# Gathers of u and v rows issued in alternating pairs in an expert layer on GpSimd

## The chip, the cores and the metric

The kernel runs on one core of one Trainium2 chip. The metric is device time in microseconds (us) of one launch. The engines are named as in the profile: PE (TensorE, matmul), DVE (VectorE), ACT (ScalarE), POOL (GpSimd), SP (SyncE, which issues the plain DMAs). Each runs its own list of instructions in program order, and they meet at semaphores.

## The reference

One block over 1024 tokens of width 1024, float32: an input projection, gated delta-net heads and sliding-window attention heads, an output projection, then a layer of single-neuron experts, then a gated per-layer embedding. The change lies in the expert layer (PEER). For each token, 8 heads pick 16 of 16384 experts each, 128 in all:

```python
def peer_experts(xn, w_query, sub_keys, expert_u, expert_v):
    ...
        eid = e1 * PEER_NKEYS + e2
        gate = jax.nn.softmax(sc, axis=-1)
        hid = jnp.einsum('thkd,td->thk', expert_u[eid], xb, preferred_element_type=f32)
        act = jax.nn.gelu(hid, approximate=False) * gate
        return jnp.einsum('thk,thkd->td', act, expert_v[eid].astype(f32)).astype(xb.dtype)
```

So for every token and each of its 128 experts one row of `expert_u` and one of `expert_v` (1024 floats each, 4 KB) are needed. That is 2 x 1024 x 128 rows, 1073.7 MB.

## The kernel before, in words

**Tiles and groups.** The tokens are cut into 8 tiles of 128, one token a partition. The 128 experts of a token are cut into 16 groups of 8 (`G = 8`, `NG = 16`). One gather (an indirect DMA) brings, for one expert slot, one row for each of the 128 tokens: 512 KB. A group has 8 gathers from `table_u` into `u_ring` (128 x 8 x 1024) and 8 from `table_v` into `v_ring`. Each ring holds one group: slot j of the next group goes where slot j of this one was.

**What is done with a group.**
- POOL, `gather_group` (L562 to L576): copies the 8 indices of each token into `ids` (L567), then issues the gathers (L576). Before an even slot it waits until the row before in that slot and the next has been used (L574), on `u_used` for u rows and `v_used` for v rows.
- DVE, `experts` (L1642 to L1648): for each slot j it waits for `u_landed[j]`, multiplies the u row by the token's input and sums it (L1645, one fused instruction, called a reduction here), which raises `u_used`. After the eighth it waits for ACT's gelu and multiplies by the gates (L1648).
- ACT, `experts`: the gelu, then eight diagonal matrices (`weight_diagonals`, 128 x 128), one for each slot, with the weights of the 128 tokens on the diagonal. Each waits for `v_used` of the slot's last user.
- PE, `experts` (L1169 to L1181): for each slot it waits for `v_landed[j]` and for the diagonal, then multiplies the diagonal by the v row in two halves (L894), into the sum `expert_sum` in PSUM. A group is 32 matmul records. Every slot raises `v_used`.

**The two halves of a tile.** While the experts of tile t-1 are computed, the same engines compute everything ahead of the experts for tile t (the "front": delta-net, attention, projections, the choice of experts), cut by hand into 16 pieces. The orders are written out by hand, and they differ by engine:

```python
# DVE, tile(t)                       # PE, tile(t)
for g in range(NG):                  for g in range(NG):
    experts(t - 1, g)                    if g:
    if g == 0:                               experts(t - 1, g - 1)
        experts_out(t - 2)               pieces[g](t)
    pieces[g](t)                     experts(t - 1, NG - 1)
publish(t)
```

ACT has DVE's order (experts of group g, then piece g). So DVE and ACT are one group ahead of PE: beside PE's experts of group g-1 stand their experts of group g, and piece g is shared by the three engines after these. Most pieces go to and fro between PE, ACT and DVE; piece 9 on PE is a projection (16 of its matmuls, `w_out_sb`) with no input from DVE or ACT in the same piece, and pieces 14 and 15 have nothing on PE. The eighth tile's experts run beside the embedding at the end (`normed_rows`, `result`, `take_pT` on DVE, `turn_rows`, `gate`, `project_p` on PE; DVE's L1718 and L1721 are in `result`).

**What sets POOL's order.** Only the code of `gather_group`, called for group after group. POOL has nothing else to do but take over the indices of a tile (`take_ids`). Where it waits for a slot, each later gather waits behind it. SP's queue has the loads of weights and of the tile's inputs and isn't touched by the change.

Of the kernel before, what the change touches and what calls it, by code (L numbers as in the profile page):

```python
# [55 lines left out]
G = 8  # L56
# [50 lines left out]
def block_kernel(nc, x, p, g_mix, w_in, gdn_conv_w, gdn_a_log, gdn_dt_bias, gdn_norm_g, swa_q_norm_g, swa_k_norm_g,  # L107
# [4 lines left out]
    sub_keys, table_u, table_v = peer_sub_keys[0], peer_u[0], peer_v[0]  # L112
# [8 lines left out]
    with ExitStack() as ctx:  # L121
        def signal(name):
            return ctx.enter_context(nc.semaphore(name))
# [51 lines left out]
        u_used = signal("u_used")  # L175
        u_landed = [signal(f"u_landed{u}") for u in range(G)]
        v_used = signal("v_used")
        v_landed = [signal(f"v_landed{u}") for u in range(G)]
# [87 lines left out]
        def sb(where, name, shape, dt=F32):  # L266
            return where.enter_context(nc.sbuf_tensor(name, shape, dt))
# [34 lines left out]
        with ExitStack() as b_ctx:  # L302
# [4 lines left out]
            u_ring = sb(b_ctx, "u_rows", [P, G, D])  # L307
            v_ring = sb(b_ctx, "v_rows", [P, G, D])
# [15 lines left out]
            ids = sb(b_ctx, "group_ids", [P, 2, G], U32)  # L324
# [236 lines left out]
        @block.gpsimd  # L561
        def _(pool):  # L562
            def gather_group(t, g, half):

                n = t * SLOTS + g * G
                first = isinstance(g, int) and g == 0 and isinstance(t, int)
                nc.gpsimd.tensor_copy(ids[:, half, :], eid[:, bass.ds(g * G, G)]).then_inc(group_ids_ready, 1)  # L567
                pool.wait_ge(group_ids_ready, t * NG + g + 1)
                pool.sem_inc(wait_carrier)
                for table, ring, used, landed in ((table_u, u_ring, u_used, u_landed), (table_v, v_ring, v_used, v_landed)):  # L570
                    for j in range(G):
                        if j % 2 == 0 and not first:

                            pool.wait_ge(used, n - G + j + 2)  # L574
                            pool.sem_inc(wait_carrier)
                        nc.gpsimd.indirect_dma_start(  # L576
                            ring[:, j, :], None, table, bass.IndirectOffsetOnAxis(ids[:, half, j:j + 1], 0)).then_inc(landed[j], 16)

            def take_ids(t):

                pool.wait_ge(vector_front, t + 1)
                pool.sem_inc(wait_carrier)
                nc.gpsimd.tensor_copy(eid[:], eid_new[:]).then_inc(ids_taken, 1)
                pool.wait_ge(ids_taken, t + 1)

            pool.wait_ge(first_ids_ready, 1)
            nc.gpsimd.tensor_copy(eid[:, 0:EARLY * G], eid_new[:, 0:EARLY * G]).then_inc(first_ids_taken, 1)  # L589
            pool.wait_ge(first_ids_taken, 1)  # L590
            for g in range(EARLY):
                gather_group(0, g, g % 2)
            take_ids(0)
            with pool.Fori(EARLY // 2, NG // 2) as pair:
                g = pair * 2
                for half in range(2):
                    gather_group(0, g + half, half)
            with pool.Fori(1, NT) as t:
                take_ids(t)
                pool.sem_inc(wait_carrier)  # L600
                with pool.Fori(0, NG // 2) as pair:
                    g = pair * 2
                    for half in range(2):
                        gather_group(t, g + half, half)
# [1156 lines left out]
```

## Time and profile before

| What | Value |
|---|---|
| Time, median of 3 runs | 4106.42 us (4103.27 to 4132.05) |
| Span of the profiled execution | 4090.1 us |
| The median run above that span | 16.3 us |
| PE busy | 3315.7 us, 81% |
| DVE busy | 2191.8 us, 54% |
| ACT busy | 992.4 us, 24% |
| POOL busy | 2278.2 us, 56% |
| DMA moved | 1214 MB, of which 1073.87 MB are the gathers |

The profile is of one execution. No time of that execution as a whole is given beside its span, so the runs' median stands for it: 16.3 us lie around the span. Expert work begins some 520 us into the span, when the first front is done, and takes the rest of it. Busy shares are means over pieces with different limits. A row of the time line gives start, duration, engine, line, operation, and in brackets how long the engine had been idle and who ended that. PE records of one kind in a row are merged, and the start of a merged row is that of its first instruction.

### The profile page before, as it was taken

Reading aid. Unit: us, or ns where it says so; the run is one execution under the profiler, and the core shown is the slowest. Engines: PE = TensorE matmul, PEld = TensorE weight load, DVE = VectorE, ACT = ScalarE, POOL = GpSimd, SP = SyncE. Lnnn points to the kernel's source line nnn. Section 1 sums busy time; section 2 is a strip of 40 time slices with the busy share of each in tenths; the row PEclk is TensorE's granted clock in tenths of the full one; section 3 lists DMA queues with packets and bytes.
Section 4 is the critical chain, followed back from the end, with each engine's and each line's share of the span. In section 5 each row is a group of like instructions: output and inputs, shape, how many; then the busy total and the mean of one; then the engine's idle time right before and its main releaser. Section 6 shows DMA issues by size and latency. Waiting matters only on the chain.

```text
span 4090.1 us, 38210 instructions
## 1 busy us (share of the span) xinstructions
PE 3315.7 (81%) x11032; PEld 1816.9 (44%) x11032; DVE 2191.8 (54%) x4881; ACT 992.4 (24%) x2278; POOL 2278.2 (56%) x2189
## 2 busy tenths in 40 slices
PE   8997757897788787887879778877888687969999
PEld 4444535453444344443535344444545253534444
DVE  1124285567444854477456744486357644574543
ACT  2112213222222132212221222212221222213332
POOL 0000055667556775767566755676566656666764
PEclk9998778898889897898889888898899798989999
DMA  3321187899789998899889978899799979999996
GB/s 125 118 75 63 39 298 263 309 363 389 264 302 335 362 358 289 316 346 365 280 313 373 365 269 297 318 360 342 278 324 369 356 260 322 352 364 373 381 355 243
DMA packets 413927, 1214.00 MB, mean 297 GB/s; under 512 B 43680, under 2 KB 137888, under 8 KB 413600
## 3 DMA queue, kind: packets, MB, share of 16 engines
q0 software_dynamic: 294912, 1073.87, 71.6%
q1 hardware_dynamic: 118816, 137.66, 9.9%
q8 instruction: 103, 1.69, 0.2%
q14 instruction: 96, 0.79, 0.1%
HBM read 1190.61 MB, written 20.77 MB: 296 GB/s over the span
## 4 chain that ended last, share of the span: by engine, by line
PE 54%; DVE 14%; issue 13%; DMA 7%; POOL 5%; ACT 4%; another core or an unknown queue 2%; SPq 1%; POOLq 0%; DVEq 0%; ACTq 0%
PE expert_sum L894 28%; PE bank L894 23%; DVE u_rows L1645 5%; DMA u_rows<-in_peer_u_dram,group_ids 4%; DMA w_query<-in_peer_w_query_dram 3%; PE bank L897 3%; POOL u_rows L576 3%; POOL v_rows L576 2%; ACT weight_diagonals L610 1%; ACT L610 1%; ACT arena L610 1%; DVE arena L1420 1%; DVE arena L1552 1%; DVE arena L1537 1%
## 5 line engine op out<-in xcount | busy, mean ns | idle before, releaser
L894 PE MATMUL expert_sum<-v_rows,weight_diagonals 128*128 128x512 f32 x4096 | 1871.7, 617 | 153.0 <-ACT weight_diagonals L610 116.9
L576 POOL DMA_INDIRECT v_rows<-in_peer_v_dram,group_ids x1024 | 1191.1, 1163 | 827.7 <-PE expert_sum L894 541.8
L1645 DVE CUSTOM_DVE_ANT_0 u_rows<-u_rows,ffn_in 128x1024 f32<-128x1024 f32 x1024 | 1215.7, 1225 | 454.8 <-DMA u_rows<-in_peer_u_dram,group_ids 410.3
L894 PEld LDWEIGHTS expert_sum<-v_rows,weight_diagonals 128*128 128x128 f32 x4096 | 810.4, 200 | 1161.7 <-issue 1078.0
L576 POOL DMA_INDIRECT u_rows<-in_peer_u_dram,group_ids x1024 | 1052.3, 1028 | 416.8 <-issue 371.0
L897 PE MATMUL bank<-constants,arena 128*128 128x128 f32 x968 | 184.5, 336 | 330.2 <-DVE arena L1475 82.4
L610 ACT ACTIVATE weight_diagonals<-constants,expert_weight 128x128 f32<-128x128 f32 x1024 | 331.7, 390 | 228.5 <-PE expert_sum L894 177.4
L894 PE MATMUL bank<-w_query,arena 128*128 128x256 f32 (+1 forms) x1088 | 297.6, 436 | 87.4 <-DMA w_query<-in_peer_w_query_dram 50.6
L610 ACT ACTIVATE gelu<-hidden 128x8 f32<-128x8 f32 x128 | 26.7, 208 | 1386.1 <-DVE hidden L1645 1237.0
L897 PEld LDWEIGHTS bank<-constants,arena 128*128 128x128 f32 x968 | 139.1, 171 | 392.6 <-issue 212.2
L894 PEld LDWEIGHTS bank<-w_query,arena 128*128 128x128 f32 x1088 | 231.6, 215 | 155.7 <-issue 59.6
L589 POOL CAST expert_id<-expert_id_new 128x32 uint32<-128x32 f32 x1 | 0.2, 209 | 522.1 <-DVE expert_id_new L1602 522.1
L894 PE MATMUL bank<-arena 128*128 128x128 f32 (+4 forms) x2176 | 252.2, 295 | 40.1 <-issue 23.0
L894 PEld LDWEIGHTS bank<-arena 128*128 128x128 f32 (+3 forms) x2176 | 240.7, 201 | 60.5 <-issue 47.0
L894 PE MATMUL bank<-w_out_sb,arena 128*128 128x512 f32 x512 | 235.2, 615 | 21.9 <-ACT arena L861 10.4
L610 ACT ACT_TABLE_LOAD x172 | 220.7, 1283 | 3.8 <-PEq L1751 0.7
L1420 DVE COPY_PREDICATED arena<-constants,bank 128x512 f32<-128x512 uint32 x80 | 58.1, 726 | 287.3 <-PE bank L894 131.6
L894 PE MATMUL bank<-normed_by_channel,w_channel 128*128 128x512 f32 x384 | 167.2, 598 | 0.5 <-issue 0.5
L894 PEld LDWEIGHTS bank<-w_out_sb,arena 128*128 128x128 f32 x512 | 99.5, 197 | 146.7 <-issue 132.7
L894 PE MATMUL bank<-w_token,normed_tile 128*128 128x512 f32 (+1 forms) x384 | 142.4, 532 | 0.0
L1513 DVE TENSOR_TENSOR arena<-arena,bank 128x512 f32<-128x512 f32 x16 | 11.0, 688 | 203.5 <-PE bank L894 173.0
L894 PEld LDWEIGHTS bank<-normed_by_channel,w_channel 128*128 128x128 f32 x384 | 73.7, 193 | 93.6 <-issue 93.6
(166 smaller groups left out, 1968.1 us busy)
## 6 DMA issues: line engine op xcount, KB each, us to landing
w_query<-in_peer_w_query_dram SPq DMA_DIRECT2D x64, 1024.0 KB
u_rows<-in_peer_u_dram,group_ids POOLq DMA_INDIRECT x1024
v_rows<-in_peer_v_dram,group_ids POOLq DMA_INDIRECT x1024
w_channel<-in_w_in_dram SPq DMA_DIRECT2D x12, 512.0 KB
conv_scratch<-conv_out SPq DMA_DIRECT2D x12, 512.0 KB, 2.6
arena<-conv_scratch SPq DMA_DIRECT2D x8, 768.0 KB
tok_scratch<-token_out SPq DMA_DIRECT2D x8, 648.0 KB
arena<-tok_scratch SPq DMA_DIRECT2D x8, 648.0 KB
```

The lines of the kernel that those rows point to most:

```text
L576: nc.gpsimd.indirect_dma_start(ring[:, j, :], None, table, bass.IndirectOffsetOnAxis(ids[:, half, j:j + 1], 0)).then_inc(landed[j], 16)
L589: nc.gpsimd.tensor_copy(eid[:, 0:EARLY * G], eid_new[:, 0:EARLY * G]).then_inc(first_ids_taken, 1)
L610: return nc.scalar.activation(out_, in_, func, **kw)
L894: return nc.tensor.matmul(out_, lhsT, rhs, start=start, stop=stop, **kw)
L897: return nc.tensor.transpose(out_, in_, ident)
L1420: v.copy_predicated(invT[:, 4 * r:4 * r + 4, :], level_mask(l), bank[3 + r][:, :].rearrange("p (s n) -> p s n", n=P)).then_inc(invT_ready, 1)
L1513: v.tensor_tensor(h1[:, n * 512:n * 512 + 512], x_t[:, n * 512:n * 512 + 512], bank[n][:, :], ALU.add).then_inc(h1_ready, 1)
L1537: last = v.max_index(index[:, first], top[:, first], row)
L1552: last = v.max_index(index[:, second], top[:, second], row)
L1645: v.tensor_tensor_reduce(u_ring[:, j, :], u_ring[:, j, :], xb[:], 1.0, 0.0, ALU.mult, ALU.add, hid[:, g * G + j:g * G + j + 1]).then_inc(u ...
```

## The change

The two loops in `gather_group` change places. Before, POOL issued the 8 gathers of u rows and then the 8 of v rows, with a wait for used slots ahead of each pair. Now it goes over the four pairs of slots, and for each pair issues two u rows and then two v rows, each two behind the same wait as before. The number of gathers, their sizes, the semaphores and the values waited for are the same. No other engine's instructions change.

```diff
-                for table, ring, used, landed in ((table_u, u_ring, u_used, u_landed), (table_v, v_ring, v_used, v_landed)):
-                    for j in range(G):
-                        if j % 2 == 0 and not first:
+                for j in range(0, G, 2):
+                    for table, ring, used, landed in ((table_u, u_ring, u_used, u_landed), (table_v, v_ring, v_used, v_landed)):
+                        if not first:
 
                             pool.wait_ge(used, n - G + j + 2)
                             pool.sem_inc(wait_carrier)
-                        nc.gpsimd.indirect_dma_start(
-                            ring[:, j, :], None, table, bass.IndirectOffsetOnAxis(ids[:, half, j:j + 1], 0)).then_inc(landed[j], 16)
+                        for i in range(j, j + 2):
+                            nc.gpsimd.indirect_dma_start(
+                                ring[:, i, :], None, table, bass.IndirectOffsetOnAxis(ids[:, half, i:i + 1], 0)).then_inc(landed[i], 16)
```

On POOL, in the loop over the groups of a tile, one group of before (`group_ids` is `ids`, `in_peer_u_dram` is `table_u`):

```order
L567 COPY group_ids<-expert_id 128x8
L568 ISA
L574 ISA
L576 DMA u_rows<-in_peer_u_dram,group_ids 128x1024 x2
L574 REGISTER_ALU
L576 DMA u_rows<-in_peer_u_dram,group_ids 128x1024 x2
L574 REGISTER_ALU
L576 DMA u_rows<-in_peer_u_dram,group_ids 128x1024 x4
L576 DMA v_rows<-in_peer_v_dram,group_ids 128x1024 x8
```

On POOL, the same group in the changed kernel (the gather's line is L577 there):

```order
L567 COPY group_ids<-expert_id 128x8
L568 ISA
L574 ISA
L577 DMA u_rows<-in_peer_u_dram,group_ids 128x1024 x2
L577 DMA v_rows<-in_peer_v_dram,group_ids 128x1024 x2
L574 REGISTER_ALU
L577 DMA u_rows<-in_peer_u_dram,group_ids 128x1024 x2
L577 DMA v_rows<-in_peer_v_dram,group_ids 128x1024 x2
L574 REGISTER_ALU
L577 DMA u_rows<-in_peer_u_dram,group_ids 128x1024 x2
L577 DMA v_rows<-in_peer_v_dram,group_ids 128x1024 x2
```

These eleven rows reach to the third pair; the fourth follows in the same way. The first pair of v rows, and the wait on `v_used` ahead of it, has moved ahead of six gathers of u rows; the last gather of u rows is now the twelfth behind that wait, itself included.

## Rows read from the trace of the kernel before

**Rows 1.** The page: its span, and part 4, the chain that ended last
```profile
span 4090.1 us, 38210 instructions
...
PE 54%; DVE 14%; issue 13%; DMA 7%; POOL 5%; ACT 4%; another core or an unknown queue 2%; SPq 1%; POOLq 0%; DVEq 0%; ACTq 0%
PE expert_sum L894 28%; PE bank L894 23%; DVE u_rows L1645 5%; DMA u_rows<-in_peer_u_dram,group_ids 4%; DMA w_query<-in_peer_w_query_dram 3%; PE bank L897 3%; POOL u_rows L576 3%; POOL v_rows L576 2%; ACT weight_diagonals L610 1%; ACT L610 1%; ACT arena L610 1%; DVE arena L1420 1%; DVE arena L1552 1%; DVE arena L1537 1%
```

**Rows 2.** The page, part 5: busy us, mean ns | idle before, and most of it
```profile
L576 POOL DMA_INDIRECT v_rows<-in_peer_v_dram,group_ids x1024 | 1191.1, 1163 | 827.7 <-PE expert_sum L894 541.8
```

**Rows 3.** Waits of the whole span: us in total, times, longest us
```profile
POOL v_rows L576 <- PE expert_sum L894: 541.8, 195, 22.7
...
DVE u_rows L1645 <- DMA u_rows<-in_peer_u_dram,group_ids: 410.3, 216, 13.3
```

**Rows 4.** Time line of PE, expert bursts of the tile from 1898 us
```profile
1898.06 13.90 PE L894 MATMUL expert_sum<-v_rows,weight_diagonals 128*128 128x512 f32 x32
...
2018.70 15.06 PE L894 MATMUL expert_sum<-v_rows,weight_diagonals 128*128 128x512 f32 x32
2042.16 15.30 PE L894 MATMUL expert_sum<-v_rows,weight_diagonals 128*128 128x512 f32 x32
2074.79 15.96 PE L894 MATMUL expert_sum<-v_rows,weight_diagonals 128*128 128x512 f32 x32
...
2130.55 13.90 PE L894 MATMUL expert_sum<-v_rows,weight_diagonals 128*128 128x512 f32 x32
2151.15 13.90 PE L894 MATMUL expert_sum<-v_rows,weight_diagonals 128*128 128x512 f32 x32
...
2335.82 4.44 PE L894 MATMUL expert_sum<-v_rows,weight_diagonals 128*128 128x512 f32 x7
```

**Rows 5.** Time line of POOL, gathers at three places of that tile
```profile
2012.58 0.94 POOL L576 DMA_INDIRECT u_rows<-in_peer_u_dram,group_ids  x1 [0.30 <-issue]
2024.27 0.94 POOL L576 DMA_INDIRECT v_rows<-in_peer_v_dram,group_ids  x1 [10.74 <-PE expert_sum L894]
2025.51 0.94 POOL L576 DMA_INDIRECT v_rows<-in_peer_v_dram,group_ids  x1 [0.30 <-issue]
...
2060.28 1.99 POOL L576 DMA_INDIRECT v_rows<-in_peer_v_dram,group_ids  x1 [0.30 <-issue]
...
2134.96 1.94 POOL L576 DMA_INDIRECT v_rows<-in_peer_v_dram,group_ids  x1 [2.91 <-PE expert_sum L894]
```

**Rows 6.** Time line of DVE, the last reduction of two groups
```profile
2021.17 1.22 DVE L1645 CUSTOM_DVE_ANT_0 u_rows<-u_rows,ffn_in 128x1024 f32<-128x1024 f32 x1
...
2061.38 1.22 DVE L1645 CUSTOM_DVE_ANT_0 u_rows<-u_rows,ffn_in 128x1024 f32<-128x1024 f32 x1
```

**Rows 7.** Two windows: us, busy by engine (x instructions), PEclk, DMA share, GB/s
```profile
2074.80:2090.80 16.00, 16.00 (x34) 6.75 (x34) 8.79 (x18) 4.56 (x11) 6.00 (x6) 0.87 0.96 331
...
1898.10:2335.80 437.70, 350.76 (x1222) 195.80 (x1221) 257.59 (x585) 105.77 (x259) 286.69 (x272) 0.89 0.92 331
```

**Rows 8.** Time lines of POOL and DVE: a group's last u gather, then its reduction
```profile
2107.13 1.49 POOL L576 DMA_INDIRECT u_rows<-in_peer_u_dram,group_ids  x1 [0.30 <-PE expert_sum L894]
...
2112.88 1.22 DVE L1645 CUSTOM_DVE_ANT_0 u_rows<-u_rows,ffn_in 128x1024 f32<-128x1024 f32 x1 [0.66 <-DMA u_rows<-in_peer_u_dram,group_ids]
...
2211.46 1.75 POOL L576 DMA_INDIRECT u_rows<-in_peer_u_dram,group_ids  x1 [0.30 <-issue]
...
2222.97 1.23 DVE L1645 CUSTOM_DVE_ANT_0 u_rows<-u_rows,ffn_in 128x1024 f32<-128x1024 f32 x1 [0.35 <-DMA u_rows<-in_peer_u_dram,group_ids]
```

**Rows 9.** Time lines of PE and DVE, two groups of the last tile
```profile
3742.77 13.90 PE L894 MATMUL expert_sum<-v_rows,weight_diagonals 128*128 128x512 f32 x32
3755.57 1.23 DVE L1721 TENSOR_TENSOR arena<-arena 128x1024 f32<-128x1024 f32 x1
3765.51 13.90 PE L894 MATMUL expert_sum<-v_rows,weight_diagonals 128*128 128x512 f32 x32
...
3789.55 13.90 PE L894 MATMUL expert_sum<-v_rows,weight_diagonals 128*128 128x512 f32 x32
```

## The prediction

> **What bounds the kernel now.** I read the page first. Of its span of 4090.1 us the chain that ended last lies 54% on TensorE (PE) and 14% on VectorE (DVE) [rows 1]. No engine is full; the bound is a chain between engines, and busy shares say little about a moved wait. Among the costliest groups stand the 1024 gathers of v rows on GpSimd (POOL), mean 1163 ns, and before them 541.8 us of 827.7 idle for PE's expert matmuls [rows 2]. 128 groups of 8 experts pass through POOL, DVE and PE. The waits say who holds whom: POOL stood those 541.8 us, in 195 waits, at v slots that PE had not used up, and DVE 410.3 us, in 216, at u rows that had not landed [rows 3]. So in the old order POOL stands still at v rows, **after** all u rows of that group are on their way.
>
> Then one tile in the order of time. Call T the start of a group's 32 expert matmuls on PE. Between 1898.06 and 2335.82 there are 16 such starts, of which the first, the last period's end and five between are shown: 437.8 us in 16 periods of 14 to 38 us [rows 4]. While PE works at group n from T = 2018.70, DVE already reduces the u rows of group n+1: their last gather was issued at 2012.58, before T, and the last reduction is over at 2022.39, 3.7 us after T [rows 5, 6]. POOL then stands 10.74 us, until 2024.27, which is T + 5.57, for the first v slots, and after the next v gather goes on at 1.24 us each [rows 5]. DVE is one group ahead of PE, and the eight early u gathers are what allows it.
>
> PE, DVE and ACT each run "experts of group n+1 (or n), then piece n+1 of the next token tile" in program order. DVE's and ACT's share of a piece stands behind their expert work of group n+1. So the next T comes a tail after the later of two ends: PE's burst, or DVE's last reduction of group n+1.
>
> **The change part by part.** It removes no gather and adds none: 16 a group stay, as do the four waits on u slots and the four on v slots. Only POOL's order changes: u0 u1, v0 v1, u2 u3, and so on. The first v wait moves ahead of six u gathers. Behind it on POOL now stand those six; for them waits DVE (the reductions of group n+1), behind DVE the gelu, the gates and the diagonals on ACT, and behind these both engines' piece. SP's queue isn't touched.
>
> When is DVE's last reduction of group n+1 over, counted from T? Four terms, whose sum I call D.
> - First v slots free: 5.6 us (2018.70 to 2024.27) [rows 4, 5]. It depends on PE's pace: behind the burst of 13.90 us the first v gather starts at T + 4.4 (2130.55 to 2134.96) [rows 4, 5], and a burst of 15.96 us had a mean granted clock of 0.87, between the levels of 1.2 and 2.4 GHz [rows 4, 7]. PE will idle more after the change, so I take the slower value and keep 4.4 as the lower bound.
> - From there u7 is the twelfth gather: v0 v1 u2 u3 v2 v3 u4 u5 v4 v5 u6 u7. Eleven steps of 1.24 and one of 0.94 make 14.6 us [rows 5].
> - Beside a reduction a gather takes 1.99 us in place of 0.94 [rows 5, 6]: 1.05 more. Six u rows are reduced while these twelve are issued, which gives 0 to 6.3 us; I take half, 3.0, since pairs land 5 us apart and a pair is reduced in 2.3.
> - From the end of u7's issue to the end of its reduction: 5.5 us where the queue was short (2108.62 to 2114.10), 11.0 where it was long (2213.21 to 2224.20) [rows 8]. POOL will have stood still ahead of these, so DMA is drained: 5.5.
>
> D = 5.6 + 14.6 + 3.0 + 5.5 = **28.7 us**. The lower end is 4.4 + 14.6 + 0 + 5.5 = 24.5, the upper 5.6 + 14.6 + 6.3 + about 7 = 33.5. The four later v waits cost nothing: PE uses up a pair each 3.5 to 4 us and POOL comes by each 5.
>
> On the third term the Trainium skill has a rule: "SBUF — State Buffer", section "Who interferes with whom", says that a VectorE instruction with two SBUF inputs contends with a GpSimd one that reads SBUF and that the loser blocks fully. The rows of 1.99 beside 0.94 agree. By the rule in full the term is 6.3 rather than 3.0; it is the second rival below.
>
> Now the tails, tile of rows 4, from the later end to the next T. Where a piece needs DVE or ACT the tail stays; where it is PE's alone it runs during the wait, and only gelu, gates and first diagonal remain: 1.0 us, as in the fourteenth and fifteenth group, which have nothing else. In order: 14.4, 14.2, 13.2, 19.0, 8.4, 12.2, 2.2, 16.4, 1.0, 16.9, 7.2, 7.1, 9.7, 1.0, 1.0, 5.3, together 149.2 us. Three of them in rows: the fifth is 2033.76 to 2042.16; the sixth runs from DVE's end at 2062.60 to 2074.79; the ninth was 6.7 us of PE alone (2144.45 to 2151.15) and falls to 1.0 [rows 4, 6].
>
> One group keeps its end: the fifteenth, whose reductions start late behind DVE's own piece and end 30.7 us after T. A tile then takes 15 x 28.7 + 30.7 + 149.2 = 610.4 us in place of 437.8: **+173**. Six tiles run so: 6 x 173 = 1038. In the last tile a pair of groups takes 22.7 + 24.0 = 46.8 us (3742.77 to 3789.55) [rows 9]. The second becomes D + 1.0 = 29.7, since what follows its burst is PE's alone; the first becomes D + 3 + 8.8 = 40.5, as PE's first transpose there waits for DVE's last product, L1721, some 3 us behind the reductions (over at 3756.80, when the burst ended too), and 8.8 us of PE and ACT follow, to 3765.51 [rows 9]. That is +23.4 a pair, seven pairs: 165. The first tile has two groups that DVE holds up anyway; I take 150 for the rest. Sum: 4090.1 + 1038 + 150 + 165 = 5443 us of span. The median run of before lies 16.3 us above the profiled span, so **5460 us**.
>
> Why no cover is left: DMA, busy 0.92 at 331 GB/s in that tile [rows 7], is the one resource near its limit. It is filled in the old order because POOL queues eight u rows ahead of its stand at v. With the stand behind two u rows the queue drains each time, and the same bytes at a tile of 610 us make 331 x 438/610 = 238 GB/s.
>
> **The rivals.**
> 1. *Faster*: u rows no longer lie in the DMA queue behind eight v rows. DVE's 410.3 us at DMA would go; the chain has 4% of the span at that wait, 164 us [rows 1, 3], so 4106 - 164 = 3942 us. It wins where the DMA queue holds a u row longer than POOL's wait for PE does. For it: issue to reduction took 11.0 us behind a full queue [rows 8]. Against: POOL's 10.74 us stand now comes ahead of six u rows and outweighs the 5.5 us that a short queue saves, in each period.
> 2. *Still slower*: each reduction blocks a gather in full, 6.3 in place of 3.0. D = 32.0, 15 x 3.3 = 50 us more a tile and about 8 tiles: 5860 us.
> 3. *No change*: v slots are free by the time POOL comes to them, so that the order doesn't matter: 4106. Against it: 195 waits, 541.8 us in all [rows 3].
> 4. *Mild*: pieces start during the wait after all, and only groups whose period is under D pay (seven of the sixteen, by 7.5 us in the mean): 52 a tile, some 440 us with the first and last tile, 4550 us. Against it: DVE's and ACT's pieces stand behind the delayed reductions in program order.
>
> **How the numbers follow.** The forecast has 0.85, rival 2 0.07, rival 4 0.04, rival 1 0.02, rival 3 0.02. What a measurement of this kernel tells from no change is about 1%. Slower by over 1%: 0.85 + 0.07 + 0.04 = 0.96, I say 0.95; within 1%: 0.03; faster: 0.02. The lower end takes D = 24.5 and 15 us a tile less in tails, since PE's first matmuls of a piece run ahead: +95 a tile, 570 + 90 + 110 = 770, so about 4870; the upper end takes D = 33.5, +245 a tile, 1470 + 190 + 220 = 1880, about 5980. I give 4850 to 5950.
>
> **What would show it.** Right: POOL's largest wait sits still at v rows for PE, with longer stands, and just ahead of them only two u rows; DVE's wait for u rows grows from 410 us to over 1000, its last reduction ending 25 to 33 us after T; PE idles about 14 us after nearly every burst; DMA falls to some 240 GB/s; GpSimd's mean gather rises above 1163 ns. Wrong: DVE's last reduction before T + 20, or shares of DMA near 0.9. If D is right and the time isn't, the tails were wrong, the granted clock first.

## The result, and the profile after

The changed kernel takes **5278.1 us** (median of 4 runs, 5249.39 to 5299.24) and the kernel before 4108.36 us (4103.27 to 4132.05) beside it: a ratio of 1.281, with a 95% interval of 1.275 to 1.287. The forecast was 5460 us in a range of 4850 to 5950. The growth is 1170 us where 1354 were forecast.

The page of the changed kernel: its span, part 1, and the two rows of part 4 (the chain that ended last), which answer to [rows 1]:

```profile
span 5279.3 us, 38210 instructions
...
PE 3411.9 (65%) x11032; PEld 1879.1 (36%) x11032; DVE 2213.8 (42%) x4881; ACT 971.2 (18%) x2278; POOL 2210.2 (42%) x2189
...
PE 37%; issue 19%; DMA 15%; POOL 14%; DVE 9%; ACT 5%; SPq 1%; POOLq 0%; ACTq 0%; DVEq 0%
PE expert_sum L895 18%; PE bank L895 17%; DMA u_rows<-in_peer_u_dram,group_ids 14%; POOL v_rows L577 8%; POOL u_rows L577 6%; DVE u_rows L1646 4%; PE bank L898 3%; ACT weight_diagonals L611 2%; ACT L611 1%; DVE arena L1421 1%; ACT arena L611 1%; ACT gelu L611 0%; DMA arena<-conv_scratch 0%; DVE expert_weight L1649 0%; DVE arena L1508 0%
```

The instructions are as many as before, and PE is busy only 96 us longer (3315.7 to 3411.9), at a mean granted clock of 0.803 of full speed in place of 0.888: the 1189 us of span are nearly all standing still. In the chain PE fell from 54% to 37%, and u rows on their way rose from 4% to 14%. GpSimd issuing gathers went from 5% to 14%. That is the forecast's path: a wait for PE on GpSimd, then gathers, then a landing, then DVE.

Part 5 of the same page, the two kinds of gathers (busy us, mean ns | idle before, and what ended most of it), for [rows 2]:

```profile
L577 POOL DMA_INDIRECT v_rows<-in_peer_v_dram,group_ids x1024 | 1060.7, 1036 | 2075.4 <-PE expert_sum L895 1808.5
...
L577 POOL DMA_INDIRECT u_rows<-in_peer_u_dram,group_ids x1024 | 1113.7, 1088 | 418.1 <-issue 345.7
```

The waits of the changed kernel (us in total, times, longest us), for [rows 3]:

```profile
DVE u_rows L1646 <- DMA u_rows<-in_peer_u_dram,group_ids: 1865.3, 453, 23.8
POOL v_rows L577 <- PE expert_sum L895: 1808.5, 164, 29.4
```

GpSimd's stand at v rows went from 541.8 us to 1808.5, in fewer and longer waits (11.0 us in the mean against 2.8). DVE's wait for u rows went from 410.3 us to 1865.3. The second is the first seen from the other side: u rows can't land that GpSimd, standing at a v row, hasn't issued.

One group in the order of time, from the fourth burst of the tile that starts at 2352.40. First PE's time line (start and duration in us; in brackets the idle time before):

```profile
2474.48 13.90 PE L895 MATMUL expert_sum<-v_rows,weight_diagonals 128*128 128x512 f32 x32
2488.22 1.95 PE L895 MATMUL bank<-arena 128*128 128x128 f32 x16
2504.00 3.78 PE L895 MATMUL bank<-arena 128*128 128x128 f32 x16 [13.84 <-ACT arena L726]
```

GpSimd's, from the first v gather of the next group:

```profile
2478.89 0.94 POOL L577 DMA_INDIRECT v_rows<-in_peer_v_dram,group_ids  x1 [18.86 <-PE expert_sum L895]
...
2487.60 1.46 POOL L577 DMA_INDIRECT u_rows<-in_peer_u_dram,group_ids  x1 [0.30 <-issue]
2489.37 1.22 POOL L577 DMA_INDIRECT v_rows<-in_peer_v_dram,group_ids  x1 [0.30 <-issue]
...
2493.38 1.24 POOL L577 DMA_INDIRECT u_rows<-in_peer_u_dram,group_ids  x1 [0.30 <-issue]
```

DVE's, the last two reductions of that group:

```profile
2497.97 1.23 DVE L1646 CUSTOM_DVE_ANT_0 u_rows<-u_rows,ffn_in 128x1024 f32<-128x1024 f32 x1 [2.89 <-DMA u_rows<-in_peer_u_dram,group_ids]
...
2499.25 1.23 DVE L1646 CUSTOM_DVE_ANT_0 u_rows<-u_rows,ffn_in 128x1024 f32<-128x1024 f32 x1
```

T is 2474.48. The first v slots come free at T + 4.4, after GpSimd has stood for 18.86 us. Twelve gathers later, at T + 20.1, u7 is issued. At T + 26.0 DVE's last reduction is over. PE ran 16 matmuls of its next piece ahead and then stood 13.84 us, until ACT, whose share of the piece lies behind all this, gave it the first block to multiply. This is no single case: between one burst and the next, PE's longest stand is over 10 us in 87 of the 96 groups of the six middle tiles, with a median of 13.1. The next burst starts at 2516.99, so the period (from the start of one burst to that of the next) is 42.5 us; from the fourth burst of the tile of before to its fifth it was 33.9 (1984.84 to 2018.70). The fourth burst of the tile of before, whose fifth is in [rows 4]:

```profile
1984.84 14.87 PE L894 MATMUL expert_sum<-v_rows,weight_diagonals 128*128 128x512 f32 x32
```

The window of that whole tile, for the second row of [rows 7] (us, busy by engine, clock, DMA share, GB/s):

```profile
2352.40:2942.80 590.40, 363.88 (x1222) 205.12 (x1221) 262.26 (x590) 104.11 (x261) 280.19 (x273) 0.78 0.68 246
```

DMA moves the same bytes at 246 GB/s, busy 0.68 of the time in place of 0.92. By the starts of tiles on PE's time line, in us:

| Tile | before | changed | growth | forecast |
|---|---|---|---|---|
| first | 443.4 | 605.5 | +162 | +150 |
| six in the middle, mean of one | 447.0 | 590.6 | +143.5 | +173 |
| last | 371.5 | 538.6 | +167 | +165 |

162 + 6 x 143.5 + 167 = 1190 us, and the spans differ by 5279.3 - 4090.1 = 1189.2.

### The profile page after: what moved, and what is told of

Its sections match the earlier page's. It is cut to its first block, busy times and chain, and to the rows that moved or that the text cites. A ratio compares the mean times of both kernels' runs of the same rounds, so it can differ in the third digit from the quotient of the medians.

```text
span 5279.3 us, 38210 instructions
## 1 busy us (share of the span) xinstructions
PE 3411.9 (65%) x11032; PEld 1879.1 (36%) x11032; DVE 2213.8 (42%) x4881; ACT 971.2 (18%) x2278; POOL 2210.2 (42%) x2189
## 4 chain that ended last, share of the span: by engine, by line
PE 37%; issue 19%; DMA 15%; POOL 14%; DVE 9%; ACT 5%; SPq 1%; POOLq 0%; ACTq 0%; DVEq 0%
PE expert_sum L895 18%; PE bank L895 17%; DMA u_rows<-in_peer_u_dram,group_ids 14%; POOL v_rows L577 8%; POOL u_rows L577 6%; DVE u_rows L1646 4%; PE bank L898 3%; ACT weight_diagonals L611 2%; ACT L611 1%; DVE arena L1421 1%; ACT arena L611 1%; ACT gelu L611 0%; DMA arena<-conv_scratch 0%; DVE expert_weight L1649 0%; DVE arena L1508 0%
## 5 line engine op out<-in xcount | busy, mean ns | idle before, releaser
L895 PE MATMUL expert_sum<-v_rows,weight_diagonals 128*128 128x512 f32 x4096 | 1909.6, 627 | 383.6 <-ACT weight_diagonals L611 329.0
L1646 DVE CUSTOM_DVE_ANT_0 u_rows<-u_rows,ffn_in 128x1024 f32<-128x1024 f32 x1024 | 1241.7, 1226 | 2026.8 <-DMA u_rows<-in_peer_u_dram,group_ids 1865.3
L577 POOL DMA_INDIRECT v_rows<-in_peer_v_dram,group_ids x1024 | 1060.7, 1036 | 2075.4 <-PE expert_sum L895 1808.5
L577 POOL DMA_INDIRECT u_rows<-in_peer_u_dram,group_ids x1024 | 1113.7, 1088 | 418.1 <-issue 345.7
L898 PE MATMUL bank<-constants,arena 128*128 128x128 f32 x968 | 203.8, 368 | 806.7 <-ACT arena L790 237.1
L895 PE MATMUL bank<-arena 128*128 128x128 f32 (+4 forms) x2176 | 277.7, 310 | 301.4 <-ACT arena L726 202.7
L898 PEld LDWEIGHTS bank<-constants,arena 128*128 128x128 f32 x968 | 158.7, 191 | 869.4 <-issue 338.7
L895 PEld LDWEIGHTS bank<-arena 128*128 128x128 f32 (+3 forms) x2176 | 263.0, 216 | 325.4 <-ACT arena L726 205.4
L895 PE MATMUL bank<-w_query,arena 128*128 128x256 f32 (+1 forms) x1088 | 277.1, 415 | 117.6 <-ACT arena L784 116.4
L895 PEld LDWEIGHTS bank<-w_token,normed_tile 128*128 128x128 f32 x384 | 73.3, 192 | 67.0 <-issue 62.5
```

What stands on the lines that cost most here:

```text
L577: nc.gpsimd.indirect_dma_start(ring[:, i, :], None, table, bass.IndirectOffsetOnAxis(ids[:, half, i:i + 1], 0)).then_inc(landed[i], 16)
L895: return nc.tensor.matmul(out_, lhsT, rhs, start=start, stop=stop, **kw)
L898: return nc.tensor.transpose(out_, in_, ident)
L1646: v.tensor_tensor_reduce(u_ring[:, j, :], u_ring[:, j, :], xb[:], 1.0, 0.0, ALU.mult, ALU.add, hid[:, g * G + j:g * G + j + 1]).then_inc(u ...
```

## The experiments

Each was run beside the kernel before on the same chip, and ratios are to that one. This matters: there were four chips in these runs, and the kernel before took 4075.42 us on the first (the first four experiments), 4069.87 on the second (the next four), but 3864.21 on the third and 3871.95 on the fourth. What divides them is the subject of the second half of this section. Edits are against the changed kernel, except those marked otherwise. D is, as in the forecast, the time from the start of a PE burst to the end of DVE's last reduction of the next group; where D or the period is given without a row, it is the mean over the 96 groups of the six middle tiles.

**Is it the place of u7 behind the first v wait?** Three other orders of the same gathers and waits. The theory says that only the number of gathers between the first v wait and u7 counts; its rival, that changing between tables costs by itself, as often as the order changes.

```diff
-                for j in range(0, G, 2):
-                    for table, ring, used, landed in (...):
+                for side, j in (("u", 0), ("u", 2), ("v", 0), ("v", 2), ("u", 4), ("u", 6), ("v", 4), ("v", 6)):
+                        table, ring, used, landed = u_side if side == "u" else v_side
```

That is the order by fours. The second has only the last u pair behind a v pair: u0 to u5, v0 v1, u6 u7, v2 to v7. The third starts with v: v0 v1, u0 u1, and so on in turn.

> Order of a group: u0 to u3, v0 to v3, u4 to u7, v4 to v7. Theory (u rows queued behind the first wait for v slots): u7 is the eighth gather behind that wait instead of the twelfth, so DVE's last reduction ends some 5 us earlier after T than in the changed kernel, at about 23 us instead of 28, and nearly every group is 5 us shorter: about 4680 us. Rival (alternation itself costs, by switches between the two tables: 1 a group before, 3 here, 7 in the changed kernel): a third of the loss, 4500 us, with gathers that take longer to land rather than later issues.

> Order of a group: u0 to u5, v0 v1, u6 u7, v2 to v7. Theory: u7 is the fourth gather behind the first wait for v slots, DVE's last reduction ends some 17 us after T, only 2 to 3 us behind PE's burst, and that part is paid in about ten of sixteen groups: about 4260 us. Rival (switches cost): 3 switches a group as with fours, so the same 4500 us as that.

> Order of a group: v0 v1, u0 u1, v2 v3, u2 u3 and so on. Theory: all eight u gathers stand behind the first wait for v slots, u7 as the sixteenth, so the last reduction ends 33 us after T, 5 us later than in the changed kernel: about 5870 us. Rival (switches cost): 7 switches a group as in the changed kernel, 5280 us.

The waits of these three, the order by fours first:

```profile
DVE u_rows L1647 <- DMA u_rows<-in_peer_u_dram,group_ids: 1391.7, 207, 22.0
POOL v_rows L578 <- PE expert_sum L896: 1289.2, 209, 27.4
```

Only the last pair behind v:

```profile
DVE u_rows L1647 <- DMA u_rows<-in_peer_u_dram,group_ids: 856.1, 283, 12.4
POOL v_rows L578 <- PE expert_sum L896: 810.0, 139, 26.1
```

v first:

```profile
POOL v_rows L578 <- PE expert_sum L896: 2630.1, 220, 38.3
DVE u_rows L1647 <- DMA u_rows<-in_peer_u_dram,group_ids: 2553.8, 594, 27.6
```

| Order | u7 is the nth gather behind the first v wait | D | period | time | ratio (95%) |
|---|---|---|---|---|---|
| last pair | 4th | 19.3 | 29.7 | 4322.0 | 1.060 (1.052 to 1.069) |
| fours | 8th | 23.8 | 32.7 | 4748.8 | 1.165 (1.160 to 1.170) |
| the change | 12th | 28.3 | 36.9 | 5278.1 | 1.281 (1.275 to 1.287) |
| v first | 16th | 33.6 | 42.2 | 5953.6 | 1.461 (1.455 to 1.467) |

Each four gathers more put 4.4, 4.5 and 5.3 us on D, where four steps of GpSimd's queue take 4 x 1.24 = 5.0 us; on the period they put 3.1, 4.2 and 5.3 us. The times came within 1.5% of what was expected. D of the mildest order was the furthest off, 19.3 us where 17 were expected. The rival falls: "fours" and "last pair" change tables equally often, three times a group, ran on the same chip and differ by 427 us. The orders in turn with u first and with v first also change tables about equally often and differ by 675 us, though on two chips. The two waits grow and shrink together in all four kernels. This is the experiment on which the explanation rests.

**Is it the wait, or the order?** Here PE multiplies by constants in place of v rows, and a v gather waits only until the last one into its slot has landed. The gathers, their bytes and PE's work stay; the wait for PE is gone.

```diff
-                            pool.wait_ge(used, n - G + j + 2)
-                            pool.sem_inc(wait_carrier)
+                            if used is u_used:
+                                pool.wait_ge(used, n - G + j + 2)
+                                pool.sem_inc(wait_carrier)
+                            else:
+                                for i in range(j, j + 2):
+                                    pool.wait_ge(landed[i], (t * NG + g) * 16)
+                                    pool.sem_inc(wait_carrier)
...
-  v_ring[:, j, n * 512:n * 512 + 512]
+  cst[:, n * 512:n * 512 + 512]
```

> The changed order, but v slots are not waited for: PE multiplies the diagonals by 512-wide pieces of the constants instead of the v rows, and a v gather waits only for the gather before it into the same slot to have landed. The product with the v rows is left out, all gathers, reductions and matmuls stay. Theory (the wait for PE ahead of six u gathers is the whole loss): as fast as the old order with the same left out, within 2%, between 3950 and 4200 us. Rival (alternation itself costs, in the DMA queue or on GpSimd): above 5000 us.

The same two edits in the old order are the control:

> The old order with the same left out (PE takes constants in place of v rows, v gathers wait only for landings): the control of the run before. Theory: 3950 to 4150 us, since in the old order the wait for v slots stands where it holds nothing that DVE needs soon. Rival: if it held something, clearly under 3900 us.

Waits of the first of the two (in turn, no wait for PE):

```profile
POOL u_rows L582 <- DVE hidden L1651: 680.7, 62, 14.4
...
DVE u_rows L1651 <- DMA u_rows<-in_peer_u_dram,group_ids: 297.0, 132, 7.4
```

In turn it took 4329.64 us, ratio 1.064 (1.056 to 1.071), with D at 12.8 where it was 28.3. Without the wait the same order has a ratio of 1.064 where the change has 1.281, and DVE's wait for u rows, 297.0 us, is even under that of before. The control took 4382.29 and 4456.28 us in its two runs, which are too far apart for an interval; the order in turn is at any rate not slower than it. So beside its control the order itself costs nothing; the order with the wait does. But I had expected 3950 to 4200 us for the first and 3950 to 4150 for the control, and both missed that. Some 6% was being lost on something new. The next kernel, which had run before these two, missed in the same way.

**Could the u gathers be kept ahead of the wait, and still alternate?** Here v of group g goes in turn with u of group g + 1: each u gather is then a group ahead of the v gathers beside it, as in the old order. The indices have a ring of four for it. This edit is against the kernel before.

```diff
+            def gather_tile(t):
+                for g in range(NG):
...
+                    if g + 1 < NG:
+                        take_group(t, g + 1)
+                    for j in range(0, G, 2):
+                        gather_pair(t, g, 1, j)
+                        if g + 1 < NG:
+                            gather_pair(t, g + 1, 0, j)
```

> v rows of group g alternate in pairs with u rows of group g+1, so the queue alternates as in the changed kernel but u keeps a lead of a group (at a tile's start the first eight u rows go first, at its end the last eight v rows go alone). Theory: alternation is harmless where u doesn't wait for the v slots of PE's preceding group: 4080 us, between 4020 and 4200. Rival (switches cost): about 5200 us, since there are as many switches as in the changed kernel.

D did fall, to 12.3, and the rival (5200 us by the changes of table) fell too. The time was 4349.07 us all the same, outside the 4020 to 4200 expected, ratio 1.065 (1.059 to 1.070). Its waits show releasers that barely appear before:

```profile
DVE arena L1431 <- remote: 260.7, 28, 14.8
ACT arena L800 <- remote: 244.8, 25, 13.3
ACT arena L725 <- remote: 185.5, 19, 14.2
```

The largest wait of that kind in the kernel before:

```profile
DVE gdn_state L1432 <- remote: 50.8, 6, 8.5
```

```profile
2084.86 1.16 PE L905 MATMUL bank<-arena 128*128 128x128 f32 x8 [1.02 <-issue]
2089.27 0.72 DVE L1431 COPY_PREDICATED arena<-constants,bank 128x512 f32<-128x512 uint32 x1 [13.02 <-remote]
2090.05 1.11 PE L908 MATMUL bank<-constants,arena 128*128 128x128 f32 x4 [4.03 <-DVE arena L1431]
2095.55 0.59 ACT L725 COPY arena<-bank 128x512 f32<-128x512 f32 x1 [10.74 <-remote]
2095.60 0.72 DVE L1431 COPY_PREDICATED arena<-constants,bank 128x512 f32<-128x512 uint32 x1 [5.61 <-remote]
```

DVE's copy at 2095.60 needs the matmuls of the row at 2084.86, which were over at 2086.02, 9.6 us earlier. ACT's copy at 2095.55 needs those of 2090.05, over at 2091.16. DVE's copy at 2089.27 needs matmuls just ahead of the first row, over 5.4 us earlier. The semaphore events of the trace say the same: the increments of the matmuls that started at 2083.57, 2085.75 and 2090.74 arrived at 2089.14, 2095.47 and 2095.53. PE had done its work; its **signal** was late. In the same microseconds GpSimd was issuing without a pause:

```profile
2086.95 0.93 POOL L576 DMA_INDIRECT u_rows<-in_peer_u_dram,group_ids  x1 [0.30 <-issue]
2088.19 0.94 POOL L576 DMA_INDIRECT v_rows<-in_peer_v_dram,group_ids  x1 [0.30 <-issue]
2089.43 0.93 POOL L576 DMA_INDIRECT v_rows<-in_peer_v_dram,group_ids  x1 [0.30 <-issue]
```

**What makes the signals late?** Two candidates: the bytes of the gathers, or the issuing. Half of each v row is gathered, in three orders: in the last kernel's, in the old one, and in the changed one. PE multiplies the half that it has twice, so its work stays.

```diff
-  ring[:, i, :], None, table, ...
+  ring[:, i, 0:512], None, table.rearrange("r (h c) -> (r h) c", h=2), ...   (v only)
...
-  v_ring[:, j, n * 512:n * 512 + 512]
+  v_ring[:, j, 0:512]
```

> The skewed order (v of group g in turn with u of group g+1), but v gathers bring 512 columns in place of 1024 and PE uses the first half twice, so a quarter of the gathered bytes is left out. The skewed run was slow although DVE ended early; its trace has 1020 us of waits that end at no work of the core, with DMA full and PE's signals arriving 3 to 9 us late. Theory (signals come late while DMA is full): these waits fall under 300 us and the time under 4100 us. Rival (the skewed order's own waits or its longer code hold it): still above 4250 us with the late signals there.

> The old order with half-width v gathers, the control of the run before. Theory: the 230 us of waits that end at no work of the core nearly go and DVE's waits for u rows shrink: 3900 to 4020 us. Rival (DMA is no part of the old kernel's time): 4060 to 4100 us as before.

> The changed order with half-width v gathers (PE uses the first half twice; a quarter of the gathered bytes is left out). It splits the 28 us to DVE's last reduction into issue and transfer. Theory (twelve gathers issued one by one after the first v slot, then one landing): issue is the same, the landing gets 1 to 1.5 us shorter, so about 5100 us. Rival (the bytes of the interleaved v rows hold the u rows up): D falls by the six half v rows, some 4 us or more, to 4700 us or below.

The first took 4321.56 us, ratio 1.062 (1.052 to 1.072), with 1008 us of "remote" waits at a mean of 218 GB/s: a quarter of the bytes gone, and nothing gained (ratio 1.065 with all of them). The theory had the waits fall under 300 us; so the bytes aren't the cause. The old order took 3995.67, ratio 0.982 (0.972 to 0.991). That is in the range expected, but not for the reason given: its "remote" waits didn't go, they are 256.5 us. The bytes are worth some 2% there, with DVE's wait for u rows at 354.6 us.

The changed order took 5304.04 us on the third chip, where about 5100 had been expected; the kernel before takes 3864.21 there, so the ratio is 1.373 (1.370 to 1.377). The changed kernel with all its bytes did not run on that chip. On its own it took 5278.1, so the times of the two agree to half a per cent, and D is 28.5 in place of 28.3. From u7's issue to the end of its reduction it is 6.4 us in place of 6.9, but from the first v gather to the end of u7's issue 16.7 in place of 15.9, since a gather took 1114 ns in the mean in place of 1062. The rival (D shorter by 4 us or more, 4700 us) fell: here the transfers are little of what is waited for, gathers in a queue are most of it.

In the last of these no signal was late at all, nor was one in the kernels that followed. Counted from the trace, a signal of a matmul is called late here if the next increment of its semaphore comes more than 1.5 us after its start. Those with none within 15 us are left out, since records are missing, so the shares are rough:

| Chip | Kernel | late, of those counted |
|---|---|---|
| of the result | before | 326 of 1614 |
| of the result | the change | 152 of 1581 |
| first | v and next u in turn | 395 of 1586 |
| second | in turn, no wait for PE | 437 of 1615 |
| second | v and next u in turn, half v | 383 of 1653 |
| third | change, half v; both with pacing, below | 0 of about 1716 each |
| fourth | v and next u in turn | 0 of 1716 |

Signals other than those of the expert bursts, split by whether GpSimd was issuing a gather within 0.5 us of the matmul's start: in the kernel before 23% of 561 were late where it was and none of 66 where it wasn't; in the changed kernel 52% of 185 and none of 488; in "v and next u in turn" 56% of 368 and 0.4% of 252. A busy DMA alone doesn't do it. Where no gather was being issued and DMA was nevertheless busy over 0.85 of the 3 us around the matmul's start, 0 of 82 of these signals were late in the changed kernel and 0 of 35 in the kernel before.

**Would pacing help?** An attempt to keep GpSimd from issuing densely: before a pair it waits until the pair two earlier has landed. Once in the old order, once in that of v and next u in turn.

> The old order, but ahead of each pair of gathers GpSimd also waits until the pair two before has landed, so that at most four rows are in flight and gathers aren't issued without gaps. Theory (PE's signals come late only while GpSimd issues gathers without gaps): waits that end at no work of the core fall from 230 to under 100 us; the time is 3980 to 4060 us. Rival (a full DMA queue is worth more than early signals): 4120 to 4250 us.

> The skewed order with the same pacing, at most four rows in flight. Theory (dense issue makes PE's signals late, and these 1020 us of waits are why the skewed order took 4349 us): they fall under 300 us and the time to 4000 to 4150 us. Rival (something else in the skewed order holds it, its longer code for example): the waits and the time stay near 4350 us.

4767.40 us, ratio 1.235 (1.232 to 1.237), and 4790.11 us, ratio 1.240 (1.238 to 1.242). Both missed by far, and neither tells anything of late signals, since that chip has none. What they show is another thing: with at most four gathers outstanding the queue runs short. In the old order DVE waits 1477.7 us for u rows, D is 24.1, and DMA is busy 0.82 of the time from 1000 to 3700 us, where in the kernel before (on the chip of the result) it is 0.90. Four outstanding are too few; depths between four and the full queue weren't tried.

**The same kernel on another chip.** The last run was the unchanged kernel of v and next u in turn.

> The skewed order once more, unchanged. The three runs before this one were on a chip where PE's signals never came late (none of some 1700 over 1.5 us) and the kernel before took 3864 us, against 4075 on the chip of the first skewed run. Theory (late signals alone made the skewed order slow): where the kernel before is near 3864 us, the skewed one is between 3780 and 3900 us, with no late signals; where it is near 4075 us, the skewed one is near 4350 again. Rival (its own waits hold it): 6% over the kernel before on either chip, near 4110 us where that takes 3864.

It took 3841.04 us (3833.49 to 3847.73), beside 3871.95 for the kernel before on that chip: ratio **0.992** (0.989 to 0.994). On the first chip the same code had lost 6.5%. The work itself is the same in both traces: the instructions of DVE add up to 2392 and 2395 us and those of ACT to 1094 and 1092, and a packet of the gathers' queue took 156 and 155 ns in the mean. What differs is the "remote" waits, 1019.7 us and none, and the granted clock, 0.873 and 0.921. Its waits, with no "remote" one among them:

```profile
DVE u_rows L1656 <- DMA u_rows<-in_peer_u_dram,group_ids: 465.2, 207, 12.8
...
POOL v_rows L576 <- PE expert_sum L905: 285.2, 117, 14.6
```

This is the one version with all its work that beat the kernel before, by 0.9%, and only on a chip without late signals. The period is 25.6 us, and DMA moves 316 GB/s over the span. The order in turn is harmless, even slightly good, once each u gather stays a group ahead of the v gathers that it stands beside. It is no version to recommend where the chip isn't known.

## Why the prediction was right, and which terms were off

**The mechanism** held in each of its steps. GpSimd's largest wait is still that for PE at v rows, and longer; DVE's wait for u rows went past 1000 us; the last reduction ends 28.3 us after T (25 to 33 was said); PE stands 13.84 us behind the burst shown and over 10 us behind 87 of 96; DMA is at 246 GB/s (238 was worked out). The three other orders show that the number of gathers behind the wait sets the loss, and the kernel without the wait shows that the wait is what sets it going.

**The terms of D**, means over 96 groups:

| Term | forecast | measured |
|---|---|---|
| T to the first v gather | 5.6 | 5.4 |
| from there to the end of u7's issue | 14.6 + 3.0 | 15.9 |
| from there to the end of u7's reduction | 5.5 | 6.9 |
| D | 28.7 | 28.3 |

Two errors of opposite sign met in D, so that it came within 0.4 us is in part luck. The **third term**, gathers slowed beside reductions, was 1.3 us in place of 3.0. Three of the twelve gathers of the group shown took 1.46, 1.22 and 1.24 us, the others 0.94, and none 1.99. GpSimd's mean gather also fell (u 1028 to 1088 ns, v 1163 to 1036, all 1096 to 1062), where I had said that it would rise above 1163. In the old order eight u rows wait in the slots and are reduced back to back; now reductions come in pairs with pauses. More gathers meet a reduction (1033 in place of 747 of the 2048), but fewer meet two in a row (335 in place of 450) and fewer take over 1.9 us (49 in place of 154). So the second rival (6.3 us, 5860 us in all) falls. On it the forecast had brought in the Trainium skill, "SBUF — State Buffer", "Who interferes with whom": by that section the loser of two such instructions blocks fully. The trace agrees only in part for the issue of a gather. Gathers that lay wholly beside reductions took 1.34 us in the mean in the changed kernel (1.49 in the kernel before) and at most 1.99, where a gather alone takes 0.94: it lost 0.4 us in the mean and never more than 1.05. The **fourth term** came out at 6.9 in place of 5.5. I had called the queue drained, but v4 and v5 (1 MB) are issued three and two steps ahead of u7 and are still in it. Over all u rows that DVE waited for, the median time from the end of the issue to the reduction's start was 5.3 us, and 4.3 us with half the v bytes, which puts about 1 us on those bytes. The forecast also speaks of four later v waits; there are three.

**The tile** was the step that failed by size: +173 forecast, +143.5 measured, six times over. 9.3 of the 29.5 us are the base: I worked with the tile of 437.8 us, the shortest of six whose mean is 447.0, and took it for all. The other 20 show in the tile of the window above, 590.4 in place of 610.4. The ends D sum to 452.2 where 461.2 were forecast (-9.0). The tails, from the end of D to the next burst, sum to 138.2 where 149.2 were (-11.0). Part of that is PE's first matmuls of a piece, which run ahead in the wait, as those at 2488.22 do; the forecast had allowed 15 us for it in the lower end alone. Another part may be fewer late signals, since the sum of "remote" waits fell from 229.6 to 18.3 us. The two weren't separated.

**First and last tile**: 162 and 167 us against 150 and 165. **Around the span**: I added 16.3 us as what lies around it. The profiled execution of the changed kernel took 5281.06 us for a span of 5279.3, so 1.8 us lie around it. The rest of the 16.3 was then the difference between executions of the kernel before. It is worth 14.5 us here.

**The other rivals.** Faster (3942) fell: DVE's wait for u rows grew instead of going. Its thought, that u rows no longer lie behind eight v rows, is right as far as it goes: for the u rows that DVE waited for, the median from the end of the issue to the reduction's start fell from 6.9 us to 5.3. But the wait ahead of them costs more. The one kernel with both tables in turn and u ahead of the wait gained 0.9% on one chip and lost 6.5% on another. "No change" fell with the ratio. Mild (4550) fell too: in the group shown the piece did not start in the wait beyond PE's first 16 matmuls, and the rest lies behind the reductions by program order.

**What stays open** is why signals are late on some chips. The chips differ, and the signals are late almost only while GpSimd issues gathers, not in step with the bytes; that is as far as the runs go. That late signals make up the whole difference between the two sorts of chips is argued and not shown: of the kernel before there is no trace on the faster ones. Whether some slower issuing that keeps the DMA queue full would be rid of them wasn't tried on a chip that has them.

## What to carry to other kernels

A queue in program order hands a wait on to all that stands behind it. Before gathers (or loads) of two streams are put in turn on one queue, ask which stream has the later wait, and how many issues of either stream will then stand between that wait and the last one of the early stream. Here each of those put 1.1 to 1.3 us, about its issue step of 1.24, on the end of the early stream's work in every group, and none of it showed in busy time. If two streams must alternate, let the one that must be early be a group ahead; here that removed the loss on one chip, and gained little. When a new kernel misses by some per cent on one chip, run it and the old one on another before the miss is explained by its code.

## What was unexpected of the hardware

- On the chips where the kernel before takes 4070 to 4108 us, signals of PE reach other engines late, by 3.7 us in the mean of those late (kernel before) and by 4.9 (v and next u in turn), if GpSimd is issuing gathers at that time. On the two where it takes 3864 and 3872 us, the traces of four kernels have not one late signal. The kernel before differs by 5 to 6% between these two sets of chips, and one and the same change (v and next u in turn) gains 0.9% on the one sort and loses 6.5% on the other.
- A wait that the profile puts down to "remote" in a program on one core was here in the main a late signal of the core's own PE (977 of 1020 us in v and next u in turn), and not another core.
- Dropping a quarter of the gathered bytes was worth only 2% in the old order, though DMA is busy 0.92 of the time in its middle tile. In the order of the change (0.68 busy) it was worth nothing that the runs show, which are on two chips.
